# A two-layer product-key expert trunk: norms with their intermediate in PSUM, Pool's subtraction in quarters, an earlier first index, other tiles turned, and expert numbers turned ahead of the coefficients

## The reference, cut to what matters

```
def peer(x, w_q, sub_keys, u_tab, v_tab):
    q = (xt @ w_q).reshape(n_tok, 8, 2, 128)                 # 8 heads, two halves of a query
    sc = einsum("thcd,hckd->thck", q, sub_keys)              # scores against 128 keys in each half
    top_s, top_i = lax.top_k(sc, 16)
    cand_s = top_s[:, :, 0, :, None] + top_s[:, :, 1, None, :]        # 16 x 16 pairs
    best_s, best_j = lax.top_k(cand_s, 16)                   # 16 experts of each head
    experts = ...                                            # row = 128 * first + second
    gates = softmax(best_s)
    h = einsum("thk,td->thk", u_tab[experts], x)             # 128 slots of each token
    coef = gates * gelu(h)
    return einsum("thk,thkd->td", coef, v_tab[experts])

x = layer_norm(ALPHA * x + mixer(x), ln_g[i, 0], ln_b[i, 0])
x = layer_norm(ALPHA * x + peer(x, ...), ln_g[i, 1], ln_b[i, 1])
```

## Time and profile before

| | us |
|---|---|
| median of 3 runs | 3581.01 |
| lowest, highest | 3579.53, 3585.43 |
| time of the profiled execution | 3584.7 |
| its span, first to last instruction | 3583.0 |

### The profile page before, as it was taken

How to read it: one execution, slowest core, us unless ns; L and a number is a source line. 1 busy time by engine, 2 the same in 40 slices (tenths; PEclk the granted TensorE clock), 3 DMA queues, 4 the chain that set the end, 5 groups by cost and what they waited for, 6 DMA issues and landing times.

```text
span 3583.0 us, 46449 instructions
## 1 busy us (share of the span) xinstructions
PE 2944.6 (82%) x15333; PEld 2268.6 (63%) x15333; DVE 2550.5 (71%) x3440; ACT 828.4 (23%) x1277; POOL 1853.8 (52%) x1464
## 2 busy tenths in 40 slices
PE   8999895767777699999399998957677777899993
PEld 7886785666767544444298976956667676544441
DVE  4986688777888776666733546797878887766667
ACT  2013331222333410000133543312223334200000
POOL 5761265777777554444200001657777775644443
PEclk9999997888899999999699999978888999999997
DMA  7432357999999589999755334469999996799998
GB/s 226 141 117 94 133 176 314 422 422 422 421 422 422 198 323 409 409 409 403 263 197 187 119 129 165 141 266 422 422 422 421 422 422 267 264 409 406 409 410 311
DMA packets 293736, 1106.87 MB, mean 309 GB/s; under 512 B 21957, under 2 KB 120837, under 8 KB 220677
## 3 DMA queue, kind: packets, MB, share of 16 engines
q0 software_dynamic: 147456, 805.37, 55.5%
q1 hardware_dynamic: 146182, 300.22, 23.3%
HBM read 1103.41 MB, written 2.10 MB: 309 GB/s over the span
## 4 chain that ended last, share of the span: by engine, by line
DMA 41%; PE 30%; DVE 15%; issue 8%; POOL 4%; ACT 1%; DVEq 0%; POOLq 0%; ACTq 0%; SPq 0%
DMA ring<-in_peer_u,index_now 20%; DMA work<-in_peer_v,index_add 12%; PE ps L640 9%; DMA more_add<-in_peer_v,index_add 8%; PE ps L660 7%; PE ps L704 6%; DVE ps L1526 3%; PE ps L829 3%; POOL ring L553 3%; DVE ring L1483 2%; DVE hot_set L1546 1%; DVE x_tok L1368 1%; PE ps L835 1%; DVE work L1432 1%; DVE work L1429 1%
## 5 line engine op out<-in xcount | busy, mean ns | idle before, releaser
L1483 DVE SCALAR_TENSOR_TENSOR ring<-ring,x_tok 128x2048 f32<-128x2048 f32 x384 | 879.5, 2298 | 227.9 <-DMA ring<-in_peer_u,index_now 220.7
L553 POOL DMA_INDIRECT ring<-in_peer_u,index_now x512 | 852.4, 1665 | 358.5 <-issue 114.3
L868 PE MATMUL ps<-all_v,mix 128*128 128x512 f32 x1984 | 851.8, 592 | 0.0
L868 PEld LDWEIGHTS ps<-all_v,mix 128*128 128x128 f32 x1984 | 377.0, 190 | 474.5 <-issue 474.5
L835 PE MATMUL ps<-x_dot,work 128*128 128x128 f32 x4096 | 534.2, 293 | 95.7 <-ACT work L1097 67.0
L1526 DVE SCALAR_TENSOR_TENSOR ps<-work,coef,ps 128x1024 f32<-128x1024 f32 x344 | 442.1, 1288 | 230.5 <-DMA work<-in_peer_v,index_add 228.5
L829 PE MATMUL ps<-ident,ring 128*128 128x128 f32 x2048 | 344.8, 339 | 313.5 <-DMA ring<-in_peer_u,index_now 308.2
L835 PEld LDWEIGHTS ps<-x_dot,work 128*128 128x128 f32 x4096 | 516.6, 208 | 117.3 <-ACT work L1097 82.7
L517 POOL TENSOR_TENSOR w_lo<-ring,w_hi 128x2048 fp32r<-128x2048 f32 x34 | 159.3, 4689 | 706.0 <-ACT w_hi L966 706.0
L829 PEld LDWEIGHTS ps<-ident,ring 128*128 128x128 f32 x2048 | 306.7, 177 | 335.9 <-DMA ring<-in_peer_u,index_now 196.8
L599 POOL DMA_INDIRECT work<-in_peer_v,index_add x312 | 294.5, 944 | 314.2 <-DVE ps L1526 249.3
(11 more groups left out here) (188 smaller groups left out, 3666.2 us busy)
## 6 DMA issues: line engine op xcount, KB each, us to landing
all_v<-in_peer_v SPq DMA_DIRECT2D x248, 512.0 KB, 6.8
ring<-in_conv_w_in SPq DMA_DIRECT2D x16, 2048.0 KB, 9.4
ring<-in_peer_w_q SPq DMA_DIRECT2D x16, 2048.0 KB, 8.2
ring<-in_attn_w_kv SPq DMA_DIRECT2D x16, 2048.0 KB, 8.6
ring<-in_conv_w_out SPq DMA_DIRECT2D x8, 2048.0 KB, 7.9
ring<-in_attn_w_q SPq DMA_DIRECT2D x8, 2048.0 KB, 8.1
ring<-in_attn_w_o SPq DMA_DIRECT2D x8, 2048.0 KB, 7.9
ring<-in_peer_u,index_now POOLq DMA_INDIRECT x512, 14.4
```

The lines of the kernel that those rows point to most:

```text
L553: pool.indirect_dma_start(u_tile(s), None, u_tab, bass.IndirectOffsetOnAxis(ap=index_now[:, half, s:s + 1], axis=0)).then_inc(u_row[s], 16)
L868: mm = pe.matmul(ps[:, dense_bank(tb, q), :], mix[tb][:, row, :], tile[:, q * 512 - HALF:(q + 1) * 512 - HALF], start=False, stop=True, sk ...
L1483: dve.scalar_tensor_tensor(out=u_tile(s), in0=u_tile(s), scalar=1.0, in1=x_tok[:, tb, :], op0=ALU.mult, op1=ALU.mult, accum_out=coef[:, tb ...
```

## The change

Six edits:

1. In `norm` the first of the two steps writes back to the PSUM banks, and the second reads it there. `x_tok` is written once.
2. Pool's `split_half` is four instructions of 512 columns instead of one of 2048.
3. `EARLY_HEADS` is 4 instead of 5: part (0, 0) of the routing stands ahead of head 4.
4. Pool waits for the first index, copies the first 8 numbers and issues the gathers of tiles 0 and 1 ahead of its last two subtractions; tiles 2 and 3 follow behind these, and tiles 4 to 7 after PE's last multiply.
5. `TURNED` is (1, 5).
6. `turn_slots` is parted. `turn_numbers` transposes the expert numbers of both blocks at once, when the routing is done, and `turn_coef` the coefficients. Masks of block 0 wait only for the numbers. In the first two groups of gathers beside them there are four batches of masks instead of two, so that all 32 are made before the last dot products. For block 1 the four masks of round 0 are made right behind the last coefficients, ahead of the wait for `residual`.

The core of the diff:

```diff
-TURNED = (3, 7)
+TURNED = (1, 5)
...
+DOUBLE = 2
...
-EARLY_HEADS = 5
+EARLY_HEADS = 4
...
-                pool.tensor_tensor(out=half_as(w_lo, u), in0=raw_half(u), in1=half_as(w_hi, u).bitcast(F32),
-                                   op=ALU.subtract).then_inc(w_split, 1)
+                whole = u in TOKEN_MAJOR[0]
+                for q in range(Q):
+                    part = slice(q * 512, (q + 1) * 512) if whole else (slice(None), slice(q * Q, (q + 1) * Q))
...
+                last.then_inc(w_split, 1)
...
                 for u in range(HALVES):
                     split_half(U_WQ[layer] + u)
...
+                    if u == HALVES - 2:
+                        pool.wait_ge(route[layer], part_at(0, 0) + PART_INDEX)
+                        pool.wait_ge(w_split, U_WQ[layer] + HALVES - 2)
+                        copy_numbers(0, 0, slice(0, U_RING), layer * (TB * GROUPS + SLOTS // 3 + 1 - OPEN_GATHERS // G_RING) + 1)
+                        for s in range(2):
+                            gather_tile(0, s, opening * 2 * NT, opening * ND)
+                pool.wait_ge(w_split, U_WQ[layer] + HALVES)
+                for s in range(2, RING):
+                    gather_tile(0, s, opening * 2 * NT, opening * ND)
+                pool.wait_ge(proj, 2 * (P_WQ[layer] + PANELS))
+                for s in range(RING, U_RING):
+                    gather_tile(0, s, opening * 2 * NT, opening * ND)
...
+                def turn_numbers():
+
+                    pe.wait_ge(route[layer], part_at(1, 1) + PART_INDEX)
+                    for tb in range(TB):
+                        for c in range(2):
+                            mm = pe.transpose(ps[:, tb, c * P:(c + 1) * P], row_e[:, tb, c, :], ident[:, :])
+                        mm.then_inc(numbers_ready, 1)
+
+                def turn_coef(tb):
+
+                    pe.wait_ge(numbers_taken, (layer + 1) * TB)
+                    pe.wait_ge(coef_done, layer * TB + tb + 1)
+                    pe.transpose(ps[:, coef_bank(tb), 0:P], coef[:, tb, :], ident[:, :]).then_inc(slot_ready, 1)
...
                 turned_dots(1, 0)
-                turn_slots(0)
+                turn_numbers()
                 turned_dots(1, 1)
-                with pe.Fori(0, GROUPS - 2) as i:
-                    mix_pair(i)
+                turn_coef(0)
+                with pe.Fori(0, DOUBLE) as i:
+                    for off in range(2):
+                        mix_pair(i, 2, off)
                     turned_dots(1, i + 2)
-                with pe.Fori(GROUPS - 2, BATCHES // 2) as i:
-                    mix_pair(i)
-                turn_slots(1)
+                with pe.Fori(2 * DOUBLE, GROUPS) as i:
+                    mix_pair(i, 1, 0)
+                    turned_dots(1, i)
+                turn_coef(1)
...
                 take_turned(1, 0)
-                take_slots(0)
+                gelu_of(0)
+                take_numbers()
+                take_turned(1, 1)
+                take_coef(0)
                 act.wait_ge(slot_taken, layer * TB + 1)
-                take_turned(1, 1)
...
-                take_slots(1)
+                gelu_of(1)
+                take_coef(1)
...
-                    dve.scalar_tensor_tensor(out=x_tok[:, tb, cols], in0=of, scalar=mv[:, tb, 0:1], in1=ln_rows[:, 0, cols],
+                    dve.scalar_tensor_tensor(out=of, in0=of, scalar=mv[:, tb, 0:1], in1=ln_rows[:, 0, cols],
                                              op0=ALU.subtract, op1=ALU.mult).then_inc(ln_steps[n], 1)
...
-                    dve.scalar_tensor_tensor(out=x_tok[:, tb, cols], in0=x_tok[:, tb, cols], scalar=lnv[:, tb, 2:3],
+                    dve.scalar_tensor_tensor(out=x_tok[:, tb, cols], in0=ps[:, Q * tb + q, :], scalar=lnv[:, tb, 2:3],
                                              in1=ln_rows[:, 1, cols], op0=ALU.mult, op1=ALU.add).then_inc(ln_steps[n], 1)
...
-                dve.wait_ge(slot_taken, layer * TB + 1)
-                for b in range(BATCHES):
-                    masks(b)
-                    if b < 28 and b % 2:
-                        dots(1, 2 + b // 2, 3 + b // 2)
+                dve.wait_ge(numbers_taken, layer * TB + 1)
+                for p in range(BATCHES // 2):
+                    masks(2 * p)
+                    masks(2 * p + 1)
+                    if p >= 2 * DOUBLE:
+                        dots(1, p, p + 1)
+                    elif p % 2:
+                        dots(1, 2 + p // 2, 3 + p // 2)
+                dve.wait_ge(numbers_taken, (layer + 1) * TB)
+                dve.wait_ge(mix_ready, (layer + 1) * BATCHES)
                 for e in range(NT):
                     last_dot(1, e)
                 weights(1)
+                mask_round(0)
...
-                dve.wait_ge(slot_taken, layer * TB + 2)
-                dve.wait_ge(x_scaled, (layer + 1) * TB)
-                dve.wait_ge(mix_ready, (layer + 1) * BATCHES)
                 for n in range(ROUNDS):
-                    for m in range(SETS):
-                        mask_set(n, m)
+                    if n:
+                        mask_round(n)
+                    else:
+                        dve.wait_ge(x_scaled, (layer + 1) * TB)
                     if n < FIRST_ADDS:
```

More of the change, by code:

```diff
@@ L524, in _, with copy_numbers, gather_tile @@
                 pool.wait_ge(w_split, U_WQ[layer])
+                def copy_numbers(half, tb, slots, copies):
+                    pool.tensor_copy(index_now[:, half, :], index[:, tb, slots]).then_inc(index_copied, 1)
+                    pool.wait_ge(index_copied, copies)
+                    pool.sem_inc(pool_tick, 1)
+                def gather_tile(half, s, turns, uses):
+                    if s in TURNED:
+                        pool.wait_ge(u_turned, turns + (2 * TURNED.index(s) + 2))
+                    else:
+                        pool.wait_ge(u_used, uses + (DOTTED.index(s) + 1))
+                    pool.sem_inc(pool_tick, 1)
+                    pool.indirect_dma_start(
+                        u_tile(s), None, u_tab,
+                        bass.IndirectOffsetOnAxis(ap=index_now[:, half, s:s + 1], axis=0)).then_inc(u_row[s], 16)
@@ new lines, in gather_group @@
+                def gather_group(tb, group, half, i=None):
+                    n = (layer * TB + tb) * GROUPS + group
+                    copies = layer * (TB * GROUPS + SLOTS // 3 + 1 - OPEN_GATHERS // G_RING) + tb * GROUPS + group + 1
+                    first = group * U_RING
+                    if i is None:
+                        copy_numbers(half, tb, slice(first, first + U_RING), copies)
+                    else:
+                        copy_numbers(half, tb, bass.ds(i * (2 * U_RING) + first, U_RING), i * 2 + copies)
+                    for s in range(U_RING):
+                        gather_tile(half, s, n * (2 * NT) if i is None else i * (4 * NT) + n * (2 * NT),
+                                    n * ND if i is None else i * (2 * ND) + n * ND)
@@ new lines, in _ @@
+                for s in range(2, RING):
[3 more added lines that the diff above has]
+                    gather_tile(0, s, opening * 2 * NT, opening * ND)
+                gather_group(0, 1, 1)
+                with pool.Fori(0, GROUPS // 4 - 1) as i:
+                    for half in range(2):
+                        gather_group(0, 2 + half, half, i)
+                for tb, part in ((0, 1), (1, 0), (1, 1)):
+                    pool.wait_ge(route[layer], part_at(tb, part) + PART_INDEX)
+                    with pool.Fori(0, GROUPS // 4) as i:
+                        for half in range(2):
+                            gather_group(tb, part * (GROUPS // 2) + half, half, i)
@@ L1054, in peer, with take_numbers, gelu_of @@
                         exp_of(layer, 0, 0)
-                def take_slots(tb):
+                def take_numbers():
+                    for tb in range(TB):
+                        act.wait_ge(numbers_ready, layer * TB + tb + 1)
+                        act.activation(by_slot[:, tb, 0:2, :], ps[:, tb, 0:2 * P].rearrange("p (a b) -> p a b", a=2), ACT.Copy) \
+                           .then_inc(numbers_taken, 1)
+                def gelu_of(tb):
                     n = layer * TB + tb
```

122 lines of the change are left out of this document (47 added, 75 removed).

## The result

| | before | after |
|---|---|---|
| median, us | 3583.22 | 3537.39 |
| lowest, highest of 4 runs | 3579.53, 3587.58 | 3532.18, 3544.91 |
| time of the profiled execution | 3584.7 | 3532.18 |
| its span | 3583.0 | 3530.4 |

The ratio is 0.9875, 95% interval 0.9856 to 0.9894: 46 us faster, where 67 were forecast.

A forecast was written before the change was run, and what follows sets the result against it. DMA engines bound the u and v stages (share 1.00 and 1.02), DVE's order of work the stretches ahead of them. Gains of 2 x 19.9 + 14.6 + 12.9 = 67.3 us from 3581.0 gave 3514 us, range 3502 to 3533.

The forecast's parts named there:

- so their length stays: u and v stages: bytes moved do not change, so both keep their length, 617 and 492 us; only their start moves.
- 33 ns is fixed cost: Pool's subtraction in quarters: each added instruction costs 33 ns, so three more cost 0.1 us a split.
- the ring: Query-weight splits: PE ends a half, ACT rounds, Pool subtracts, PE starts its pair; three turns to head 3 add 0.3 us.
- two and a half waits: 3 us: Routing part (0, 0) on DVE: blocked instructions wait for Pool's quarters some two and a half times, 3 us; part 12.7 us.
- my bound of 7.2: Routing part (0, 0): upper bound on DVE's waits, six instructions with two SBUF tensors at 1.2 us each.
- Rival A: Opening: quarters dearer and DVE more blocked than taken; opening gives 12 to 16 us, 3521 to 3529; chance 0.17.
- rival D: u stage: refills of turned tiles too late, PE late behind mix pairs; 3592 at 8 us late; chance 0.04.
- over a stage that already holds two routing parts: u stage: argument against late refills, DMA share is 1.00 although two routing parts of 9.66 us stand on DVE.
- Rival E: DMA stages: they start earlier, but the DMA share falls inside them; ends near 3581; chance 0.02.
- Some 19 of the 19.9 us: Gather groups with doubled masks: DVE's dots, eight masks and two small diagonals fill some 19 of 19.9 us.
- covered on DVE: Gather groups with doubled masks: the extra work fits on DVE; PE 0 to 2 us late in two groups.
- The tail: End of u stage: round 1 of the masks begins 14.6 us earlier after the last landing in layer 0, 12.9 in layer 1.

The follow-up runs named there:

- late quarters: Changed kernel with Pool's splits in quarters only for the last eight of sixteen halves of each layer's query weights, the rest whole: 3534.8 us.
- the parts moved: Changed kernel with DVE's routing parts (1, 0) and (1, 1) moved from behind tile 7's dot to behind the following tile 0's dot: 3534.0 us.

## Why the prediction was right or wrong

Two steps failed: the routing part's waits in the opening, and "so their length stays" for the u stage. The opening's error by itself (11.4 us) would have left the time near 3525, inside the range. The u stage's 12.3 us took it out.

*Edit 1 was right*: 8.5 us, shown alone and together.

*Edit 2 was mis-sized.* "33 ns is fixed cost" came from comparing the shortest of another kind of Pool instruction (L583) with an eighth of a split. It is 0.14 to 0.15 us for each added instruction: a split takes 4.60 us in one piece, 5.03 to 5.05 in four and 5.59 in eight. To head 3 the ring paid 1.3 us instead of 0.3.

*Edit 3's part was mis-sized*, and this is the larger term: "two and a half waits: 3 us". It was 7.3 (16.97 against 9.64 of part (0, 1)), just above my bound of 7.2. Two things failed. I counted only instructions with two SBUF tensors (4.1 us in fact); the `tensor_scalar` ones with a single input are blocked too (3.2 us). And I multiplied by Pool's busy share, while from the first multiply to the end of the index work Pool's eight pieces run back to back, and nearly every instruction that can be blocked meets one. The page "SBUF — State Buffer" of the Trainium skill, section "Who interferes with whom", says that copies, casts and `tensor_scalar` can take the path shared with GpSimd in a two-port mode, and that reductions never do. The trace agrees for two of these: the `tensor_scalar` L1490 takes 1.18 us against 0.20, and the reduction L1485 1.22 in both places. I had not used it. Rival A described this (an opening of 12 to 16 us) with chance 0.17, and measured were 13.9 and 14.5. Of the 6.0 us missing in layer 0, about 4.3 are the part, 1.4 lie up to head 3 and 0.4 behind the part.

*Edit 5 in the u stage: the step that failed.* "Nothing in this change alters how many bytes these two move, so their length stays": the bytes did stay, their rate did not. Against rival D I had put that the share is 1.00 "over a stage that already holds two routing parts". That held because tile 7 was PE's. A part then began behind tile 6's dot, one landing ahead of tile 0. With tile 7 a DVE dot, the part begins one tile, 2.5 us, later, and so does the refill of tile 0: Pool's first gather behind part (1, 0), in the timeline of before and then of after:

```profile
723.81 2.23 POOL L553 DMA_INDIRECT ring<-in_peer_u,index_now  x1 [7.08 <-DVE ring L1483]
```

```profile
709.13 2.44 POOL L546 DMA_INDIRECT ring<-in_peer_u,index_now  x1 [9.60 <-DVE ring L1533]
```

Pool waits 2.5 us longer for DVE's dot of tile 0. That this is the cause is shown by turning tiles 1 and 5 in the kernel before (the dips appear, u stage 5.9 and 3.9 us longer), by turning 3 and 7 in the changed kernel (dips gone), and by moving the parts (most of the dip gone). Rival E had said that the DMA share would fall inside the stages, with chance 0.02; it fell in the u stage alone, and cost 12.3 us, not the whole gain.

*Edit 6's doubled masks.* "Some 19 of the 19.9 us" and "covered on DVE" summed busy times and left out that two mask buffers make the third batch wait for PE. In the profiled execution of the changed kernel this did not yet cost DMA time: the 4.6 and 7.7 us of its u stage are edit 5's, as far as the windows show. With the parts' dip removed it cost 3 to 4.5 us in each layer. Rival D's mechanism, PE late at tile 1 behind its mix pairs, is there too (1.68 us), beside DVE's wait (5.98 us), which it did not have; it counted the loss in 16 groups, and it comes in two. With both causes removed the u stage is 619.4 and 620.3 us, so 0.4 and 2.5 us more than before are left; in layer 1 the windows show 2.2 us of DMA loss, whose cause stays open. (Rival D's sum is off as well: 2.5 us in 32 groups are 80, so by its own terms 8 us late is 3594, not 3592.)

*The tail was right*: 15.5 and 11.7 against 14.6 and 12.9. Layer 1's shortfall is in the residual, and there in TensorE's clock. In layer 0 the residual ran at a granted clock of 1.00, that is 2.4 GHz, and took 3.60 us. In layer 1 the same eight matmuls took 5.29 us. Around them the windows of the kernel after are:

```profile
2964.00:2966.00 2.00, 0.16 (x2) 0.19 (x3) 1.56 (x8) 0.31 (x1) 1.70 (x2) 1.00 0.08 12
2966.00:2968.00 2.00, 2.00 (x5) 0.89 (x5) 2.00 (x4) 1.55 (x5) 1.44 (x2) 0.76 0.83 268
2968.00:2972.00 4.00, 4.00 (x14) 2.09 (x12) 0.82 (x2) 0.00 (x0) 2.12 (x3) 0.69 0.90 311
2972.00:2976.00 4.00, 2.60 (x21) 2.23 (x20) 4.00 (x6) 2.36 (x7) 2.70 (x3) 1.00 0.46 135
```

PE was busy 0.16 of 2 us ahead of the fall, and back at 1.00 behind 2972; 0.76 and 0.69 are means over time at 2.4 and at 1.2 GHz. In layer 0 it was nearly as idle (0.32 of 2 us) and kept its clock, so the traces don't say what decides. Nor does it belong to layer 1: with late quarters the residual took 5.29 us in layer 0 and 3.60 in layer 1, and with the parts moved 3.60 in both. The tail's gain thus varies by 1.7 us in a layer from kernel to kernel.

*Edit 4* was costed rightly in kind: no gain, but without it the dots wait (1.97 us for tile 2) and the opening is 1.8 us longer. Its place in Pool's order was not the one that the forecast costed (see the result).

## What to carry to other kernels

When a resource is saturated over a long stage, ask not whether it stays saturated on average but which release each refill waits for, and move nothing by even one tile without redoing that count. Cutting a blocking instruction into pieces pays only near the instructions that it blocks; elsewhere each piece only adds its cost to the ring. Work that is doubled in a slot has to be spread (doubled buffers were not tried), whatever the sum of busy times says. A stall can hide a second one, so look again when the first is gone. And two edits that remove the same stall do not add.

## What of the hardware was not expected

A DVE instruction with 64 columns and one input stood 1.0 us behind a Pool piece of 512 columns, and 0.5 us behind one of 256. Between back-to-back pieces DVE usually got in after one. In two places of all runs it did not: once it waited for all four quarters, 4.9 us (2295.76 us, above), and once for three eighths, 2.1 us (519.84 us, above). What decides between these was not tried.
